# Transposes two chunks and value products three chunks behind a head's scores

## The reference

```python
h = _rms_norm(x, g_pre_mix)
qa, ka, va, qb, kb, vb = _project(h, w_in, pos)            # one projection, partial rotary
num, m, l = _banded(qa, ka, va, WINDOW_A)                  # mixer A: 16 heads, 2 key heads, window 128
o_a = _sink_normalise(num, m, l, attn_sinks)
o_b = _merge_dilations([_dilated_prompt(qb, kb, vb, w, d) for w, d in DILATIONS])   # mixer B: 16 heads
o = jnp.concatenate([_rms_norm(o_a, g_out_a), _rms_norm(o_b, g_out_b)], axis=-1)
x = x + _rms_norm(o @ w_out, g_post_mix)
x = x + _rms_norm((gelu(causal_dwconv3(h2 @ w_gate)) * (h2 @ w_up)) @ w_down, g_post_ffn)
```

## Time and profile before

| | us |
|---|---|
| median of 3 runs | 1316.21 (1312.35 to 1316.63) |
| profiled execution | 1318.04 |
| its span, first to last instruction | 1316.2 |
| PE matmuls busy | 1214.8 (92%) |
| DVE busy | 776.2 (59%) |
| ACT busy | 571.0 (43%) |
| POOL busy | 203.2 (15%) |
| DVE, low part of a chunk (line 723), mean of 364 | 1.288 |

### The profile page before, as it was taken

How to read it: one execution, slowest core, us unless ns; L and a number is a source line. 1 busy time by engine, 2 the same in 40 slices (tenths; PEclk the granted TensorE clock), 3 DMA queues, 4 the chain that set the end, 5 groups by cost and what they waited for, 6 DMA issues and landing times.

```text
span 1316.2 us, 24517 instructions
## 1 busy us (share of the span) xinstructions
PE 1214.8 (92%) x9403; PEld 1186.3 (90%) x9403; DVE 776.2 (59%) x993; ACT 571.0 (43%) x938; POOL 203.2 (15%) x134
## 2 busy tenths in 40 slices
PE   5998777888989897999999999999999999999994
PEld 5987776787879897999999999999999999999994
DVE  5657859676554557655655556555565544454445
ACT  4334344436544456544444444444444433343331
POOL 2053525260200020000101001010010000020003
PEclk9998978888978998999999999999999999999997
DMA  6676969695522454455555555555555665656541
GB/s 252 224 242 222 295 195 285 204 255 155 150 75 82 139 172 117 146 184 183 170 168 188 184 182 169 167 189 185 180 171 166 216 185 179 177 181 184 176 144 66
DMA packets 83166, 237.03 MB, mean 180 GB/s; under 512 B 7432, under 2 KB 32368, under 8 KB 82032
## 3 DMA queue, kind: packets, MB, share of 16 engines
q1 hardware_dynamic: 81728, 232.30, 56.9%
q0 software_dynamic: 1072, 3.90, 0.9%
q10 hardware_dynamic: 320, 0.20, 0.1%
HBM read 231.13 MB, written 5.20 MB: 180 GB/s over the span
## 4 chain that ended last, share of the span: by engine, by line
PE 80%; DVE 8%; issue 3%; DMA 3%; ACT 3%; POOL 1%; SPq 0%; ACTq 0%; DVEq 0%; POOLq 0%
PE ps L1161 25%; PE ps L1162 24%; PE ps L1163 24%; DVE wl L723 2%; DMA raw<-in_w_in 2%; DVE bSc L873 1%; DVE bP L885 1%; PE ps L1225 1%; DMA Pb<-p_dram 1%; PE ps L1224 1%; ACT Pb L585 1%; PE ps L1233 1%; DVE sh L734 1%; POOL Kd L1073 1%; DMA qb<-q_dram 1%
## 5 line engine op out<-in xcount | busy, mean ns | idle before, releaser
L1161 PE MATMUL ps<-hh,wh 128*128 128x264 f32 x2080 | 609.3, 293 | 22.0 <-DVE wl L723 16.1
L1163 PE MATMUL ps<-hh,wl 128*128 128x264 f32 x2080 | 601.2, 289 | 0.0
L723 DVE TENSOR_TENSOR wl<-raw,wh 128x1024 fp32r<-128x1024 f32 x364 | 462.8, 1288 | 200.0 <-ACT wh L502 199.8
L1162 PE MATMUL ps<-hl,wh 128*128 128x264 f32 x1952 | 566.3, 290 | 0.0
L502 ACT CAST wh<-raw 128x1024 fp32r<-128x1024 f32 x364 | 375.4, 1045 | 356.9 <-PE ps L1163 298.5
L1161 PEld LDWEIGHTS ps<-hh,wh 128*128 128x128 f32 x2080 | 403.2, 194 | 31.7 <-DVE wl L723 17.5
L1163 PEld LDWEIGHTS ps<-hh,wl 128*128 128x128 f32 x2080 | 401.8, 193 | 0.0
L1162 PEld LDWEIGHTS ps<-hl,wh 128*128 128x128 f32 x1952 | 377.8, 194 | 0.2
L1162 PE MATMUL ps<-gl,wh 128*128 (+1 forms) x704 | 200.4, 285 | 0.0
L1161 PE MATMUL ps<-gh,wh 128*128 (+1 forms) x704 | 199.9, 284 | 0.0
L1163 PE MATMUL ps<-gh,wl 128*128 (+1 forms) x704 | 199.5, 283 | 0.0
(11 more groups left out here) (210 smaller groups left out, 1085.4 us busy)
## 6 DMA issues: line engine op xcount, KB each, us to landing
raw<-in_w_gate SPq DMA_DIRECT2D x88, 512.0 KB, 3.7
raw<-in_w_up SPq DMA_DIRECT2D x88, 512.0 KB, 4.6
raw<-in_w_down SPq DMA_DIRECT2D x88, 512.0 KB, 3.9
raw<-in_w_in SPq DMA_DIRECT2D x68, 512.0 KB, 6.9
raw<-in_w_out SPq DMA_DIRECT2D x32, 512.0 KB, 3.7
Pb<-p_dram SPq DMA_DIRECT2D x16, 642.0 KB, 8.5
Vd<-in_vb SPq DMA_DIRECT2D x8, 1280.0 KB, 8.5
Kd<-in_kb SPq DMA_DIRECT2D x8, 1024.0 KB, 5.9
```

Source lines behind the costliest of these rows:

```text
L723: V.tensor_tensor(wl[:, slot], raw[:, slot], wh[:, slot].bitcast(F32), ALU.subtract).then_inc(lo_ready, 1)
L1161: nc.tensor.matmul(out, a, x, start=start, stop=False)
L1162: nc.tensor.matmul(out, a, xl, start=False, stop=False)
L1163: return nc.tensor.matmul(out, b, x, start=False, stop=stop)
```

## The change

Two lines of the table of distances `STEP` (line 103). T was placed one chunk behind S and V two; now T stands two and V three behind, for all eight groups. Stage O is placed relative to V, and moves one chunk too. No instruction is added or taken away.

```diff
 STEP = {
-    "T": [1, 1, 1, 1, 1, 1, 1, 1],
-    "V": [2, 2, 2, 2, 2, 2, 2, 2],
+    "T": [2, 2, 2, 2, 2, 2, 2, 2],
+    "V": [3, 3, 3, 3, 3, 3, 3, 3],
```

## The result

| | us, median (lowest to highest) |
|---|---|
| before, 4 runs | 1314.28 (1311.97 to 1316.63) |
| after, 4 runs | 1335.82 (1334.58 to 1340.58) |
| ratio after to before | 1.0171, 95% interval 1.0136 to 1.0205 |
| profiled execution after | 1340.58, its span 1338.8 |

The change makes the kernel 1.7% slower, 21.5 us by the medians. The forecast of 1335 was 0.8 us off; the increase that it forecast, 19.3 us, was 2.2 us too small, and the fourth run of the kernel before moved that median down by 1.9, so part of the closeness is luck.

What follows compares the result with a forecast made beforehand. PE (matmuls 92% busy) was taken as the bound, mixer B's waits as DVE's and the ring's. Mixer A +10.7, clock +11, mixer B -2.4 gave +19.3 us on the 1316.21 median: 1335 us, range 1314 to 1351.

Steps and rivals of the forecast that it cites:

- Mixer B: First four groups, ahead of chunk 57: most PE waits stay under another name; -2.4 us, ends -8 and +3.
- the sum of the new waits: PE's waits before chunk 57 on DVE's low part, `evac` and PT's copy behind `bV`: about 25 to 35 us.
- the waits of V behind `bV`: Chunk 29, V1.0 waits for T1.0 behind `bV1`, some 6.6 us; `bV3` does the same to V2.0, 5.3 us.
- the count to 168.4 against 169.2: PE reaches `qk2` at 168.4 us, `evac7` ends at 169.2; PE's idling in chunks 30 and 33 covers the delay.
- The ring: Path through POOL's `mul`, DVE, DRAM and `qk`; T and V touch it once, at most 0.8 us in three groups each.
- Mixer A: Last four groups, from chunk 57: O falls behind other work on DVE; +10.7 us without the clock, +11 with clock.
- The term of chunk 76: O7 comes behind the sample tokens' stage, low part and `evac20`; N1 needs it, so W1.0 starts later: +6.4 us.
- The term for more V and T: Chunks 74 and 75 get a V and a T more, as heads end a chunk later: +1.2 us.
- The clock: PE runs at half clock after each of four new mixer A waits: 6.4 to 17.6 us, taken as +11.
- The waits go: Rival: DVE and the ring move up with PE, 41.7 us go and mixer A's 21.7 come: 1296 us; chance 0.10.
- It cancels: Rival: mixer B gains 12 us and the clock costs only 4: +3, 1318 us; chance 0.08.
- The cover fails: Rival: in mixer B, V behind `bV1` and `bV3` delays the ring, twice 6 us; +15 with clock, 1350; chance 0.12.

Runs made afterwards that it cites:

- mixer B alone: Kernel before with T 2 and V 3 in mixer B's four groups only, mixer A at 1 and 2: 1312.03 against 1316.24 us, ratio 0.9978.
- POOL short: Kernel before with POOL's products cut to one of eight sample tokens: 1285.11 against 1315.63 us; with T 2, V 3 in mixer B as well, 1286.55.
- O early: Mixer A's O directly behind the group's last V: on changed kernel 1306.65 us (0.9922), on kernel before 1307.14 (0.9939), both against 1316.24.

## Why the prediction was right

**Mixer B.** The step was: the waits change their name. This is shown in the profile of after, and by the run with mixer B alone: -0.2% (-0.4% to 0.0%), where the forecast had -2.4 us, 0.2%. What was mis-sized is the sum of the new waits. I wrote 25 to 35 us; they were 43.7 in after and 38.5 in mixer B alone. I had named the waits of V behind `bV` (6.6 and 5.3 us; V1.0's measured 5.75, V2.0's 6.19) but not added them. They cost no time, since PE's slack there took them, as the count to 168.4 against 169.2 said. The start of chunk 57 moved by +1.9 us in the profiled execution, within the 3 us that were forecast. Over all profiles it did not move: with the old distances in mixer B it lies at 298.59, 297.94 and 298.60 us, with the new ones at 300.50, 296.00, 297.91 and 296.50. The -2.4 us are neither confirmed nor refuted.

**The ring.** That POOL's products and DVE behind them set much of the pace is shown by the 30 us. That they are all of it is not: the forecast had ACT and DVE waiting for POOL, and with POOL short the DMA of the weights is what they wait for. The forecast of the time didn't need it, but the reason given for the waits was only part of the reason. One sentence of the forecast is also too wide: not every DVE instruction that reads SBUF operands stands still while POOL multiplies. This reduction in the kernel before reads `Kd` from SBUF and ran beside POOL's product of 95.13 (5.64 us long) for 3.35 us, its length also where POOL is short; the low part right behind it took the 4.12 us of the earlier trace rows:

```profile
94.46 3.35 DVE L873 TENSOR_REDUCE bSc<-Kd 128x48 f32<-128x3072 f32 x1 [6.68 <-POOL Kd L1073]
```

**Mixer A**, term by term, forecast and trace of after:

| chunk | term | forecast | measured |
|---|---|---|---|
| 64 | V5.0 waits for O4 | 5.2 | 5.18 |
| 68 | V6.0 waits for O5 | 3.4 | 3.22 |
| 72 | V7.0 waits for O6 | 2.6 | 2.43 |
| 76 | W1.0 waits for O7 and N1 | 6.4 | 5.35 |
| 63, 67 | V5.0 for O4, V6.0 for O5: gone | -4.3 | -4.3 |
| 60 | W0.0 waits longer for N's scaling | none | 0.7 |
| 74, 75 | a V and a T more | 1.2 | in the next row |
| | clock, net of chunk 67 (PE's busy time) | 7.2 | 8.2 |
| 57 to 84 | all of mixer A | 21.7 | 20.8 |

The term of chunk 76 was 1.1 us too large: the matmuls of chunk 76 ran at half clock for longer (5.65 us from first to last, against 4.6 before), and so covered more of N1. The term for more V and T had no ground in this stretch. The waits of chunks 63 and 67 went as forecast. That the cause is O's place on DVE was shown by undoing it alone: the four waits and two old ones go with one line.

**The clock** was the largest unknown, 6.4 to 17.6 us. The value taken, 11, came from the two rows and from choosing within them by whether a slow stretch lay there already. The four stretches held 8.00 + 5.99 + 6.82 + 5.37 = 26.2 us of PE's work at half clock, so 13.1 were lost; the one that went had held 8.48, 4.2 lost where 3.8 were forecast. That the net of 7.2 met the measured 8.2 so closely is luck, since against the execution with mixer B alone it would be 12.2.

**O early** gave 10 us on the changed kernel where 5 were expected, and 8 on the kernel before where 8 were. The 5 had 2 us of loss in mixer B and 1 for the V and T taken off; the run with mixer B alone and the matmuls of the stretch show neither. Without them 8 were to be expected, and the rest lies within the interval.

**The rivals.** "The waits go" falls with mixer B alone. "It cancels" had the right size for neither part. "The cover fails" did not happen, though its place came within 0.8 us of it.

## What to carry to other kernels

A wait in the profile names the first instruction of an in-order queue that misses something; what is late may be something that the next ones need too. Before moving it, look up when the next instruction in that queue could start; here that was 1.6 to 2 us earlier, not 8.8.

A step that is moved takes along what is placed relative to it. The heads' T and V were harmless a chunk later; the small stage behind them, 1.3 us on DVE, came behind other work and cost about 21 us through four waits and the clock. Place such a stage by what is ahead of it in its engine's queue, directly behind its input if it is short.

## What I had not expected of the hardware

With POOL's products an eighth as long, DVE's busy time ahead of chunk 57 fell from 211 to 160 us with the same instructions, and the granted clock's mean over the span rose from 0.955 to 0.969. But ACT's waits for the weights' DMAs doubled, from 25.4 to 53.7 us. With one wait shortened, the next one in the same queue came to light.

In the sample tokens' 32 matmuls of 16 columns in chunk 75 the granted clock fell to half without any wait of PE's ahead of it. In the kernel before, PE was busy throughout; the two rows are the stretches on either side of the fall:

```profile
415.60:419.05 3.45, 3.45 (x26) 3.20 (x24) 0.00 (x0) 2.50 (x6) 0.00 (x0) 1.00 0.03 13
419.05:422.50 3.45, 3.45 (x15) 3.22 (x14) 0.00 (x0) 3.36 (x8) 0.00 (x0) 0.50 0.00 0
```
